# A streaming encoder step on TensorE: the SBUF start of the operand regions moved to three places of 128 bytes, and thirty spare products behind the last one

## The reference, cut to what matters

```python
h = x @ w_in                                     # (576, 2048) x (2048, 5124)
y_A = RG_LRU(causal_conv4(x_branch)) * gelu(gate)
y_B = chunk_band_attention(...)                  # 4 heads
y_C = forgetting_attention(...)                  # 4 heads
x = LN1(alpha * x + concat(rms(y_A), rms(y_B), rms(y_C)) @ w_out)
x = LN2(alpha * x + relu(x @ w_up)**2 @ w_down)  # (576, 2048) x (2048, 8192) and back
```

## The kernel before, in words

| space | holds of the moving operands | before | after the change |
|---|---|---|---|
| `extra` | y_hi_b | 96 | 64 |
| `resid` | F4 | 96 | 64 |
| `region_x` | y_hi, F6, F5 | 96 | 0 |
| `acc` | y_lo, F7, F3 | 96 | 0 |
| `region_h` | F1, F2 | 96 | 32 |

## Time and profile before

### The profile page before, as it was taken

The page is one execution under the profiler, slowest core; times in us unless marked ns, Lnnn a source line. Parts: engine busy times, 40 slices in busy tenths (PEclk is TensorE's granted clock), DMA queues, the critical chain, the costliest instruction groups (busy, mean ns, idle before and its releaser), DMA issues.

```text
span 2264.6 us, 38827 instructions
## 1 busy us (share of the span) xinstructions
PE 2246.3 (99%) x16556; PEld 2195.6 (97%) x16556; DVE 1719.4 (76%) x1314; ACT 1046.0 (46%) x1050; POOL 254.7 (11%) x273
## 2 busy tenths in 40 slices
PE   9999999999999999999999999999999999999998
PEld 8999999998889999999999999999999999999997
DVE  5667899885567766767777778778778878878887
ACT  4434566554444456654444444454345235335243
POOL 2010212210111032000000000001112102112101
PEclk9999999999999999999999999999999999999999
DMA  9775766776444487674555455679689789769875
GB/s 289 251 227 163 211 170 188 211 218 221 147 141 131 151 265 227 196 252 150 185 166 183 147 174 169 203 245 241 174 237 244 189 221 260 192 164 292 236 211 178
DMA packets 423343, 459.60 MB, mean 203 GB/s; under 512 B 16376, under 2 KB 398368, under 8 KB 422696
## 3 DMA queue, kind: packets, MB, share of 16 engines
q1 hardware_dynamic: 342608, 358.22, 50.3%
q0 software_dynamic: 36080, 52.64, 13.2%
q10 hardware_dynamic: 44520, 46.80, 6.1%
HBM read 371.12 MB, written 88.05 MB: 203 GB/s over the span
## 4 chain that ended last, share of the span: by engine, by line
PE 86%; DVE 5%; DMA 4%; ACT 2%; issue 1%; SPq 0%; ACTq 0%; DVEq 0%
PE psum L3097 55%; PE psum L2823 17%; PE psum L3066 4%; PE psum L513 4%; DMA raw<-in_w_down 2%; PE psum L3041 1%; DVE w_lo L2153 1%; PE psum L2903 1%; PE psum L2986 1%; PE psum L3002 1%; DVE x_e_lo L2293 1%; DVE w_lo L1706 1%; PE psum L2815 1%; PE psum L2982 0%; DMA kc<-in_cache_band_k 0%
## 5 line engine op out<-in xcount | busy, mean ns | idle before, releaser
L3097 PE MATMUL psum<-x_e_hi,w_hi 128*128 128x288 f32 x1600 | 474.6, 297 | 1.0 <-DVE w_lo L2153 0.8
L3097 PE MATMUL psum<-x_e_hi,w_lo 128*128 128x288 f32 x1600 | 474.2, 296 | 0.0
L3097 PE MATMUL psum<-x_e_lo,w_hi 128*128 128x288 f32 x1600 | 466.8, 292 | 0.0
L3097 PE MATMUL psum<-x_b_hi,w_hi 128*128 128x288 f32 x1536 | 455.4, 296 | 2.6 <-DVE w_lo L2153 1.2
L3097 PE MATMUL psum<-x_b_hi,w_lo 128*128 128x288 f32 x1536 | 455.3, 296 | 0.0
L3097 PE MATMUL psum<-x_b_lo,w_hi 128*128 128x288 f32 x1536 | 447.9, 292 | 0.0
L3097 PEld LDWEIGHTS psum<-x_e_lo,w_hi 128*128 128x128 f32 x1600 | 304.8, 190 | 0.0
L3097 PEld LDWEIGHTS psum<-x_e_hi,w_hi 128*128 128x128 f32 x1600 | 300.7, 188 | 2.7 <-DVE w_lo L2153 2.3
L3097 PEld LDWEIGHTS psum<-x_e_hi,w_lo 128*128 128x128 f32 x1600 | 300.0, 187 | 0.0
L3097 PEld LDWEIGHTS psum<-x_b_lo,w_hi 128*128 128x128 f32 x1536 | 292.8, 191 | 0.1
L3097 PEld LDWEIGHTS psum<-x_b_hi,w_hi 128*128 128x128 f32 x1536 | 288.6, 188 | 3.9 <-issue 2.0
(11 more groups left out here) (434 smaller groups left out, 4859.7 us busy)
## 6 DMA issues: line engine op xcount, KB each, us to landing
raw<-in_w_down SPq DMA_DIRECT2D x61, 1024.0 KB, 7.1
raw<-in_w_up SPq DMA_DIRECT2D x54, 1024.0 KB, 6.5
raw<-in_w_in SPq DMA_DIRECT2D x34, 1024.0 KB, 7.2
a_even<-in_w_down SPq DMA_DIRECT2D x30, 1024.0 KB, 7.2
raw<-in_w_out SPq DMA_DIRECT2D x24, 1024.0 KB, 5.5
a_even<-in_w_up SPq DMA_DIRECT2D x24, 1024.0 KB, 6.8
h_scratch<-c_tile ACTq DMA_DIRECT2D x48, 288.0 KB, 2.3
down_scratch<-c_tile POOLq DMA_DIRECT2D x45, 288.0 KB, 5.0
```

What stands on the lines that cost most here:

```text
L3097: mm = pe.matmul(PS[:, bank, 0:HALF], w, x[:, k, :], start=(k + n == 0), stop=(k == UK - 1 and n == 2))
```

## The change

Three sizes of unused filling move the four spaces, two small constants share one tile (so that all still fits), and thirty products are appended behind TensorE's last one, into PSUM banks 0 to 3, which nothing reads any more. They take F5's hi part and `w_hi` as operands, whatever lies there.

```diff
-        sb("align_64_bytes", [128, 18])
+        sb("align_64_bytes", [128, 10])
...
         R = sb("resid", [128, KT, TOK])
 
+        sb("line_gap_x", [128, 16])
         r = Region()
         XR1 = r.sb("x_rows_1", [128, 3, D])
...
         ACC = sb("acc", [128, KT, TOK])
 
+        sb("line_gap_h", [128, 8])
         r = Region()
         r.sb("sigma_too", [128, 2 * UK * UC])
...
-        gelu0, half = sb("gelu_0", [128, 1]), sb("half", [128, 1])
+        two = sb("gelu_0_and_half", [128, 2])
+        gelu0, half = two[:, 0:1], two[:, 1:2]
...
+            pe.wait_ge(rows_c, 20)
+            spare_x, spare_w = (t[0][:, :, :].rearrange("p k c -> p (k c)") for t in (F5, WH))
+            for bank, (n, w_cols, x_at, w_at) in enumerate(((288, 128, 0, 0), (288, 128, 32, 0), (288, 128, 16, 0), (288, 128, 8, 0), (512, 128, 0, 0), (64, 128, 0, 0))):
+                for _ in range(5):
+                    pe.matmul(PS[0:w_cols, bank % 4, 0:n], spare_w[:, w_at:w_at + w_cols], spare_x[:, x_at:x_at + n], start=True, stop=True)
```

## The result

The changed kernel takes **2277.22 us** (median of 6 runs, 2275.09 to 2277.55) against 2268.66 us for the kernel before (6 runs): a ratio of 1.0033, 95% interval 1.0023 to 1.0043. It is slower by 8.6 us. I had forecast 2184 us, 85 us faster, and gave slower a chance of 0.10.

What follows compares the result with a forecast made beforehand. TensorE's own pace was taken as the bound, 3777 products in 500 us. A gain of 94.7 us less 10 given back took 85 off the 2264.6 us span, giving 2180, plus 3.6 for 2184 us; range 2155 to 2271.

Steps and rivals of the forecast that it cites:

- The bound: Whole kernel: TensorE's own pace sets the end, 3777 products in 500 us, one in 132.4 ns.
- The step that failed: TensorE's moving operand is read in whole 128-byte pieces: ten from place 96 (133.3 ns), nine from place 0 (120 ns).
- The term of 94.7 us: 9568 products whose moving operand goes from place 96 to place 0 save 9.9 ns each, 94.7 us in all.
- an end piece used again: Where blocks follow one another in one run, a shared end piece was supposed to save 1.0 ns a product.
- The rival "no change": All full-rate products: the 12 ns may be a price of the full rate itself, whatever the address; 2268 us, chance 0.25.
- The rival on the other side: Slower: weights and 9568 moving operands both begin at place 0, readers meet, 1.1 ns each, 10.5 us; 2279 us, chance 0.10.
- Places 64 and 32: 2080 products moved to 64 and 4064 to 32 still touch ten pieces: no change; bounds 0 to 22.7 and 4 us.
- From span to time: Device time was taken to lie 3.6 us above the profiled span, turning 2180 into 2184 us.
- Given back: The weight split must keep up with shorter units; waits return 10 us of the gain, with 0 and 20 as ends.
- Thirty products: Appended behind TensorE's last product, they take 4.1 to 4.4 us, hidden under ScalarE's last transfer; cover 2.2 us, cost nothing.
- VectorE and transfers at other places: VectorE, ScalarE and transfers working on tiles at new places: no change in time.
- lines of 16 bytes: A skill page's rule against the forecast: only crossing into a new 16-byte line costs, so the gain would be 0.

Runs made afterwards that it cites:

- the third set of series: Kernel before with spare products appended behind its last one, weights and moving operands read from several places; 132.2 to 133.8 ns a product with 128 weight columns.

## Why the prediction was wrong

**The bound: right.** TensorE's own pace sets the end, before and after; in the stretch of the earlier trace rows nothing else moved.

**The step that failed** is the reading of that pace: "If the reader of the moving operand takes whole pieces of 128 bytes ... ten cost 133.3 and nine 120." It rested on one ratio, 10/9, seen at one place only. The term of 94.7 us (9568 products, 9.9 ns each) was of the wrong sign: F5, F6, F7 and F3 went from 132.2 to 133.3 (8256 products), and the 1280 products of the output projection changed by half a nanosecond at most. In its place: passing over 1152 bytes takes 126.7 to 127.2 ns at all four places (bfloat16, every second element), 9.1 bytes per ns, and float32r with a weight load of 128 columns beside it 5 to 8 ns more, by the distance of the two. 133.3 turned up again at place 0, where nine pieces are touched, so the match of the ratio was chance or has another ground. And the 1.0 ns between F3 and F4, put down to an end piece used again, turns round with the place: at 0 F4 is the faster one (132.3 against 133.3).

**The evidence that I passed over.** Two rows spoke to it. The plain float32 products excluded a large fixed cost, and rightly; they did not tell "slower bytes" from "one piece more". And the forget products, whose weights step through all four places: I read their mean of 133.1 ns as "the stationary operand's place seems not to matter". It is the mean over four distances, and the four with the moving operand at 96 in the third set of series, (133.0 + 133.8 + 132.5 + 132.2) / 4, give 132.9. A mean over all cases cannot show that the cases are equal.

**The rival "no change"** (0.25) had the better reason for the 12 ns, a price of the full rate itself: some 7 ns go to the bytes and 5 to 8 come on top (126.7 less 120, and the float32r paces less 126.7). That this holds "whatever the address" is wrong by 1 to 2 ns, which is the 8.6 us.

**The rival on the other side** came out near, in part by luck. It said that operands of 9568 products come to lie at the weights' own place and pay 1.1 ns each, 10.5 us, 2279 us. Measured 2277.2, and its condition (a pace above 132.3 in F5 to F7) is met. It had 0.10, "nothing in the rows shows that the two readers disturb each other"; the 1.1 ns between F3 and F4 were such a sign. Right was that the place relative to the weights counts. But reading "in the same pieces" is not what the runs show, as distance 32 is as slow or slower and F4 is slowest at 96. Its count missed in both directions: the output projection's 1280 products did not pay, F1 and F2 at 32 did (4032 products, 1.1 ns each in the large stage and 1.6 in the input projection), and F4 at 64 gained 0.6 (1.1 us). In all some 12288 x 1.1 - 1.1 = 12.4 us, of which 10.3 appear in the span.

**Places 64 and 32.** "No change" was roughly right for F4 (-0.6 ns) and wrong for F1 and F2 (+1.1).

**From span to time.** The sum added 3.6 us, the distance of a median from one quick execution. Nearly all executions that list both have 1.7 to 1.8; at this size it changes nothing.

**Given back** did not arise: no unit became shorter. **Thirty products:** cover of 2.2 us forecast, about 2.4 left over, cost nothing: right. Their 512 columns took 230 ns and more, not 216, by the same 0.44 ns a column. **VectorE and transfers at other places:** nothing, right.

**The pages.** The Trainium skill (SBUF — State Buffer, Door 1: The DMA port swizzle) with its lines of 16 bytes says nothing that would give the change: every place in it is a multiple of 16, and the pace went from 132.2 to 133.3 ns. Starts 4 or 8 bytes off a multiple of 16 cost 3 ns more, which is the direction of such lines, but place 112 with blocks 2304 apart, a multiple of 16, cost as much (135.4). So the runs do not bear that line length out for TensorE. The Trainium skill (TensorE: Matmul & The Clock Gate, Step-by-step: what each phase is for) says that loading weights does not take read bandwidth from a running matmul. The runs disagree: with 32 weight columns instead of 128 the same product went from 131.9 to 128.9 ns, and the weights' place alone, 0 against 64, moved the triples from 132.2 to 133.8.

## What to carry to other kernels

A ratio that fits to the digit, seen at one setting, is a guess: before a sum is built on it, find a row at a second setting, and give the reading a chance no larger than its rivals' where there is none. Where TensorE streams float32r operands at full rate, reckon with 0.44 ns a column and 5 to 9 ns a product instead of one cycle a column (an estimate from the series of 256 to 512 columns). Placing operands in SBUF is worth 0.1 to 0.6% here, it goes for the most part by the distance between weights and moving operand, and a filling that is right for one layout is wrong as soon as something ahead of it changes.

## What the runs showed of the hardware that I had not expected

- Float32r moving operands at the full clock come at 0.44 ns a column (256 to 512 columns); bfloat16 of 288 columns takes 122.6 ns, the same spread over 1152 bytes 126.7 to 128.3, float32r with every second column 257 to 259.
- The pace depends on the distance of the two operands' starts within 128 bytes: 132.2 (96), 132.2 (64), 133.3 (0), 133.3 to 134.5 ns (32) with blocks 1152 bytes apart, and 133.3, 132.7, 132.3, 131.9 with blocks 2304 apart. The two kinds want different distances; why was not found.
- Below 256 columns the pace of float32r stops falling: the series of 192 columns takes (2309.19 - 2307.37) / 16 = 114 ns, 112 inside it, and those of 128 and 64 columns 112 too. The load of 128 weight columns may set it; no short series had fewer.
- A pattern of starts repeats every 12 products (of 127 to 138 ns at distance 96) and goes on over unit borders; its cause stays open.
